# Folding the pooling branch's maps into the output projection's rows, once a layer, instead of a product in each tile

## The chip, the cores and the metric

The kernel runs on 1 core of one Trainium2 chip. The metric is the device time of one execution in microseconds (us). The program works in f32 throughout; TensorE's records show each f32 matmul (and each transpose, which is a matmul with the identity) as two instructions.

## The reference, cut to what matters

Two layers work on 2048 tokens of width 1024. In each, the normalised input is projected to 2048 columns, of which 256 (`u_b`) belong to the pooling branch. Three branches give a vector `mix` of 1024 channels (512 attention, 256 pooling, 256 retention), and `w_out` maps it back:

```python
def multiscale_pool(u, pool_w, pool_scale):
    ...
        mean = (c - shifted) / jnp.minimum(t1, float(w))
        outs.append(mean - uf[..., sl])
    d = jnp.stack(outs, axis=2)
    y = jnp.einsum('bsgc,gce->bsge', d, pool_w.astype(jnp.float32)).reshape(b, s, POOL_WIDTH)
    return (y * pool_scale.astype(jnp.float32)).astype(u.dtype)
...
        mix = jnp.concatenate([y_a, y_b, y_c], axis=-1)
        x = x + jnp.einsum('bse,ed->bsd', mix, w_out[l])
        x = x + moe_ffn(rms_norm(x, norm_ffn[l]), router_w, router_b, w_gate[l], w_up[l], w_down[l])
```

`pool_w` holds four 64x64 maps a layer, `pool_scale` 256 numbers. Between `d` and the sum over `w_out`'s rows 512 to 767 all is linear, so map and scale can also be multiplied into those rows. `moe_ffn` sends each token to 2 of 32 experts.

## The kernel before, in words

A layer has a mixing part and an expert part. The mixing part takes the tokens in 16 tiles of 128 and is a software pipeline written out by hand: `steps` runs `step(s, b, front, back, tail)` for s = 0 to 17. `front` is tile s (input projection, in four chunks of 512 columns), `back` is tile s-1 (attention, pooling, retention, output projection), `tail` is tile s-2 (router). Steps 0, 1, 14, 15, 16 and 17 are written out, steps 2 to 13 are a loop of two. Step 0 has no back, step 16 no front, step 17 only a tail. Each engine runs its own program in its written order, and semaphores tie them together; a wait holds all that stands behind it on that engine.

On TensorE (L1059 to L1248) a step issues, in order: transposes of q, k and the retention's rows; chunk 0; scores; transposes for the router; chunk 1; the first half of chunk 2; L1171 to L1191, the retention's products and the pooling sums (`d` of the reference, transposed, in `bB[:, 256:512]`); the second half of chunk 2; L1198, transposes of the attention's probabilities; L1203, the pooling map, two matmuls; the first half of chunk 3; L1216, probabilities by values; L1220, transposes of `yc`; the second half of chunk 3; L1239, the output projection, in two halves k of eight matmuls of 128x512, over the blocks `d` of `mixT` and `wout`. Blocks 4 and 5 are the pooling branch. Between the two halves stand the router's rank products and the transposes of the next tile's normalised input (`hn_transposes`).

On ScalarE (L612 to L672) the order around the change is: L655 (third chunk out of PSUM), L659 (transposed probabilities), L663 (mapped pooling, with the scale, into `mixT[:, 4:6]`, which raises `pool_ready`), L667 (fourth chunk), L670 (attention into `mixT[:, 0:4]`, which raises `attn_ready`), L672 (sum of squares). On VectorE L826 copies the pooling sums from PSUM to `dT` and raises `kvd_read`.

`par` holds a layer's small parameters, with the maps `pw` (L187, two blocks of 128x128 with two maps each on the diagonal) and the scale `pscale`. `wout` (L182) has a layer's whole `w_out`, loaded during step 0. The PSUM banks are `bA` to `bF` and `bIP0`, `bIP1`; the projections use the last two, the rest of a step the others.

Of the kernel before, what the change touches and what calls it, by code (L numbers as in the profile page):

```python
# [21 lines left out]
P = 128  # L22
# [31 lines left out]
ALU = mybir.AluOpType  # L54
# [80 lines left out]
def small_parameters(norm_mix, norm_ffn, q_norm, k_norm, sinks, pool_w, pool_scale, router_w, router_b):  # L135

    both = lambda a: np.concatenate([a, a], 1)[:, :, None]
    per_chunk = lambda a: a.reshape(DEPTH, -1, P).transpose(0, 2, 1)

    heads = sinks.reshape(DEPTH, 2, 2, 2).transpose(0, 2, 3, 1)  # L140
    heads = np.broadcast_to(heads[:, :, None, :, :, None], (DEPTH, 2, 64, 2, 2, 2)).reshape(DEPTH, P, 8)
    maps = np.zeros((DEPTH, 2, 64, 2, 2, 64), pool_w.dtype)
    for g in range(4):
        maps[:, g % 2, :, g // 2, g % 2] = pool_w[:, g]
    maps = maps.reshape(DEPTH, P, 2 * P)
    router = np.broadcast_to(router_w.reshape(DC, P, NE).transpose(1, 0, 2).reshape(1, P, DC * NE), (DEPTH, P, DC * NE))
    bias = np.broadcast_to(router_b.reshape(1, 1, NE), (DEPTH, P, NE))
    return np.ascontiguousarray(np.concatenate(
        [per_chunk(norm_mix), per_chunk(norm_ffn), both(q_norm), both(k_norm), heads, maps,
         per_chunk(pool_scale), router, bias, by_quarters(norm_ffn, 1).reshape(DEPTH, P, DC)], 2))  # L150


def program(nc, x, small, w_in, w_out, w_gate, w_up, w_down, consts_d, rot_d, pads_d, out):
# [4 lines left out]
    with ExitStack() as ctx:  # L158
# [47 lines left out]
        def part(phase, n):  # L206
            at = used[phase]
            used[phase] = at + n
            assert used[phase] <= ARENA, used
            return arena[:, at:at + n]  # L210
# [16 lines left out]
        v0w = [part("mix", 128) for _ in range(2)]  # L227
        upv = [part("mix", 256) for _ in range(2)]
        iT = part("mix", 512).rearrange("p (h n) -> p h n", h=4)
        dT = part("mix", 256).rearrange("p (j n) -> p j n", j=2)  # L230
        logits4 = dT[:, 0]
        state = [part("mix", 128).rearrange("p (j e) -> p j e", j=2) for _ in range(2)]
        kv = part("mix", 128).rearrange("p (j e) -> p j e", j=2)
        ysq, z = (part("mix", 256).rearrange("p (a j e) -> p a j e", a=2, j=2) for _ in range(2))
# [32 lines left out]
        inner_ready, pe_h2T, h2T_ready, pe_router = sem("inner_ready"), sem("pe_h2T"), sem("h2T_ready"), sem("pe_router")  # L267
        pe_ykv, kvd_read, ysq_ready, z_ready = sem("pe_ykv"), sem("kvd_read"), sem("ysq_ready"), sem("z_ready")
        exp_gate, silu_ready, yc_ready = sem("exp_gate"), sem("silu_ready"), sem("yc_ready")
        pe_pT, pT_ready, pe_lin, pool_ready = sem("pe_pT"), sem("pT_ready"), sem("pe_lin"), sem("pool_ready")  # L270
        pe_ycT, ycT_ready, pe_pv, attn_ready = sem("pe_ycT"), sem("ycT_ready"), sem("pe_pv"), sem("attn_ready")
        vw_ready = sem("vw_ready")
        pe_oproj, x_new = sem("pe_oproj"), sem("x_new")
# [322 lines left out]
        def _(e):  # L596
# [6 lines left out]
            with e.Fori(0, DEPTH) as l:  # L603
# [8 lines left out]
                def step(s, b, front, back, tail):  # L612
                    t0 = l * TILES + s
                    o = 1 - b
                    if back:

                        e.wait_ge(pe_qkrT, t0)
                        for g in range(2):
                            a(qT[:, g].rearrange("p c j n -> p j c n"),
                              bC[:, 256 * g:256 * g + 256].rearrange("p (j c n) -> p j c n", j=2, c=2), ACT.Copy, scale=qgs[:, 0:1])  # L620
                        a(kTr[:, :, :, o], bD[:, 0:256].rearrange("p (g c n) -> p g c n", g=2, c=2), ACT.Copy,
                          scale=kg).then_inc(qkT_ready, 1)
                        e.wait_ge(proj_ready, t0 * 4)
                        a(eg, proj[o][:, RG0:RG0 + RW], ACT.Exp, scale=-1.0).then_inc(exp_gate, 1)
                    if front:
                        if has_next(s):
                            e.wait_ge(hn_ready, t0 + 1)
                            sumsq_front(s + 1, o)
                        e.wait_ge(proj_psum, t0 * 4 + 1)
                        a(proj[b][:, 0:512], bIP0[:, :], ACT.Copy).then_inc(proj_ready, 1)  # L630
                    if back:

                        e.wait_ge(neg_max, t0)
                        for k in range(2):
                            for g in range(4):
                                n = 4 * k + g
                                a(pr[:, k, g], (bC, bD)[k][:, g * P:(g + 1) * P], ACT.Exp, bias=stat[:, 16 + n:17 + n],  # L637
                                  scale=1.0, accum_out=stat[:, 24 + n:25 + n])
                        a(stat[:, 40:48], stat[:, 32:40], ACT.Exp).then_inc(exp_done, 1)
                    if front:  # L640
                        e.wait_ge(proj_psum, t0 * 4 + 2)
                        a(proj[b][:, 512:1024], bIP1[:, :], ACT.Copy).then_inc(proj_ready, 1)
                    if tail:
                        e.wait_ge(pe_parts, t0 - 1)
                        a(logits4, bA[:, 0:P], ACT.Copy).then_inc(parts_read, 1)
                        e.wait_ge(pe_router, t0 - 1)
                        a(es, bA[:, 256:288], ACT.Exp, scale=-1.0).then_inc(exp_router, 1)
                    if back:
                        e.wait_ge(pe_ykv, t0)
                        for k in range(2):  # L650
                            a(ysq[:, k], (bE, bF)[k][:, 256:384].rearrange("p (h e) -> p h e", h=2), ACT.Square)
                        e.drain().then_inc(ysq_ready, 1)
                    if front:
                        e.wait_ge(proj_psum, t0 * 4 + 3)
                        a(proj[b][:, 1024:1536], bIP0[:, :], ACT.Copy).then_inc(proj_ready, 1)  # L655
                    if back:
                        e.wait_ge(pe_pT, t0)
                        for k in range(2):
                            a(prT[:, k].rearrange("p g n -> p (g n)"), (bC, bD)[k][:, :], ACT.Copy)  # L659
                        e.drain().then_inc(pT_ready, 1)  # L660
                        e.wait_ge(pe_lin, t0)
                        for j in range(2):
                            a(mixT[:, 4 + j], bB[:, j * P:(j + 1) * P], ACT.Copy, scale=pscale[:, j:j + 1])  # L663
                        e.drain().then_inc(pool_ready, 1)
                    if front:
                        e.wait_ge(proj_psum, t0 * 4 + 4)
                        a(proj[b][:, 1536:2048], bIP1[:, :], ACT.Copy).then_inc(proj_ready, 1)  # L667
                    if back:
                        e.wait_ge(pe_pv, t0)
                        a(mixT[:, 0:4].rearrange("p j n -> p (j n)"), bF[:, :], ACT.Copy).then_inc(attn_ready, 1)  # L670
                        e.wait_ge(x_new, t0 * 2)
                        a(squares, xr[o], ACT.Square, accum_out=stat[:, 4:5]).then_inc(sumsq_2, 1)  # L672
# [33 lines left out]
        def _(e):  # L706
# [38 lines left out]
            with e.Fori(0, DEPTH) as l:  # L745
                e.wait_ge(par_full, (l + 1) * 16)

                v.tensor_scalar(qgs[:, :], qg, HD ** -0.5, None, ALU.mult)
                v.tensor_copy(base[:, :], const("slot0"))
                v.memset(state[0], 0.0)  # L750
# [17 lines left out]
                def step(s, b, front, back, tail):  # L768
# [53 lines left out]
                    if back:  # L822

                        e.wait_ge(pe_ykv, t0)
                        v.tensor_tensor(kv, bB[:, 0:128].rearrange("p (j e) -> p j e", j=2), state[o], ALU.add)
                        v.tensor_copy(dT, bB[:, 256:512].rearrange("p (j n) -> p j n", j=2))  # L826
                        e.drain().then_inc(kvd_read, 1)
                        v.tensor_tensor(state[b], kv, bc(const("gamma").unsqueeze(2), [P, 2, HD]), ALU.mult)

# [216 lines left out]
        def _(e):  # L1046
# [8 lines left out]
            with e.Fori(0, DEPTH) as l:  # L1055
# [3 lines left out]
                def step(s, b, front, back, tail):  # L1059
# [39 lines left out]
                    if not front:  # L1099

                        e.wait_ge(rank_read, t0 - 1)
                        e.wait_ge(pool_ready, t0 - 1)
                    if back:

                        if not first:
# [88 lines left out]
                    if back:  # L1194
# [3 lines left out]
                                i = tr((bC, bD)[a][:, g * P:(g + 1) * P], pr[:, a, g])  # L1198
                        i.then_inc(pe_pT, 1)

                        wait_alone(e, kvd_read, t0)
                        for j in range(2):
                            i = mm(bB[:, P * j:P * j + P], pw[:, j], dT[:, j], start=True, stop=True)  # L1203
                        i.then_inc(pe_lin, 1)
                    chunk(3, (0, 4))
                    if back:
                        e.wait_ge(pT_ready, t0)
# [17 lines left out]
                    if back:  # L1225

                        e.wait_ge(wout_full, (l + 1) * 16)
                        e.wait_ge(pool_ready, t0)
                        for k in range(2):
                            if front:  # L1230
                                e.wait_ge(proj_ready, t0 * 4 + 3 + k)
                            elif k == 0:
                                e.wait_ge(x_new, (t0 - 2) * 2 + 2)
                            for n, d in enumerate((4, 5, 0, 1, 2, 3, 6, 7)):
                                if n == 2 and k == 0:
                                    e.wait_ge(attn_ready, t0)
                                if n == 6 and k == 0:
                                    e.wait_ge(ycT_ready, t0)
                                i = mm(bIP[k][:, :], mixT[:, d], wout[:, d, 512 * k:512 * k + 512], start=(n == 0), stop=(n == DC - 1))  # L1239
                            i.then_inc(pe_oproj, 1)  # L1240
                            if k == 0 and tail:
# [76 lines left out]
```

## Time and profile before

| what | us |
|---|---|
| median of 3 runs | 3396.63 (3395.2 to 3398.5) |
| the profiled execution | 3395.41 |
| its span, first to last instruction | 3393.6 |
| TensorE busy | 3236.3 (95%) |
| VectorE busy | 1483.2 (44%) |
| GpSimd busy | 1086.7 (32%) |
| ScalarE busy | 579.8 (17%) |
| mean granted TensorE clock | 0.974 of 2.4 GHz |

All rows come from one execution. L numbers are lines of the kernel before. PE is TensorE, PEld its weight loads, DVE VectorE, ACT ScalarE, POOL GpSimd. Matmuls overlap their neighbours in the records, so what a group costs is the distance from its start to the next group's start, not its own duration.

### The profile page before, as it was taken

The numbers are of one execution on the slowest core, as the hardware profiler recorded it, in microseconds if no ns is written. First come the engines' busy times: TensorE is split into PE (matmuls) and PEld (weight loads), VectorE is DVE, ScalarE is ACT, GpSimd is POOL, SyncE is SP. The second block draws the span as 40 slices with busy tenths as digits, with TensorE's granted clock in tenths as the row PEclk, the third lists the DMA queues.
The fourth block names the chain that finished last, engine by engine and source line by source line (L and its number), as shares of the span: only waits on it lengthen the run. The fifth ranks groups of instructions, "written<-read, shape, count | busy, mean of one in ns | idle before, by whom it ended". The sixth has DMA issues, their size and how long they took to land.

```text
span 3393.6 us, 57969 instructions
## 1 busy us (share of the span) xinstructions
PE 3236.3 (95%) x19892; PEld 2437.0 (72%) x19892; DVE 1483.2 (44%) x4776; ACT 579.8 (17%) x1728; POOL 1086.7 (32%) x1093
## 2 busy tenths in 40 slices
PE   8999999999499999999889999999994999999998
PEld 4555555555399999999845555555553999999998
DVE  3566666666322222222235666666663222222221
ACT  1212122122011111111112121222220111111111
POOL 1011111111155455554410111111111554555643
PEclk9999999999699999999989999999996999999999
DMA  6101111011288899999831011010122888999996
GB/s 260 57 29 56 45 39 56 28 56 61 105 306 289 281 319 328 343 345 344 279 120 57 29 56 56 28 56 35 50 78 107 298 287 283 323 331 340 342 345 189
DMA packets 209896, 596.94 MB, mean 176 GB/s; under 512 B 61368, under 2 KB 101816, under 8 KB 176696
## 3 DMA queue, kind: packets, MB, share of 16 engines
q1 hardware_dynamic: 146904, 510.75, 39.7%
q0 software_dynamic: 62720, 82.95, 11.2%
q8 instruction: 124, 2.03, 0.2%
q14 instruction: 148, 1.21, 0.1%
HBM read 514.37 MB, written 80.35 MB: 175 GB/s over the span
## 4 chain that ended last, share of the span: by engine, by line
PE 91%; DVE 2%; DMA 2%; issue 2%; POOL 1%; DVEq 1%; ACT 0%; SPq 0%; POOLq 0%; ACTq 0%
PE bank L1264 27%; PE bank L1077 26%; PE bank L1290 14%; PE bank L1239 13%; PE bank L1052 4%; DMA arena<-hrows,arena 1%; PE bank L1191 1%; PE bank L1216 1%; PE bank L1135 1%; POOL arena L570 1%; POOL out L577 1%; PE bank L1144 1%; PE bank L1159 1%; DVE arena L1005 0%; DMA out<-arena 0%
## 5 line engine op out<-in xcount | busy, mean ns | idle before, releaser
L1264 PE MATMUL bank<-arena,wts 128*128 128x135 f32 (+6 forms) x8192 | 1026.0, 287 | 45.2 <-DVE arena L1008 45.2
L1264 PEld LDWEIGHTS bank<-arena,wts 128*128 128x128 f32 x8192 | 1019.7, 191 | 45.5 <-issue 45.5
L1077 PE MATMUL bank<-wts,arena 128*128 128x512 f32 x2048 | 916.8, 596 | 3.6 <-DVEq L763 3.6
L1077 PEld LDWEIGHTS bank<-wts,arena 128*128 128x128 f32 x2048 | 376.3, 191 | 416.0 <-issue 412.2
L577 POOL DMA_INDIRECT out<-arena x316 | 512.8, 1623 | 148.3 <-issue 89.9
L1290 PE MATMUL bank<-arena,wts 128*128 128x135 f32 (+6 forms) x4096 | 516.6, 287 | 2.6 <-DVE arena L1032 2.4
L1290 PEld LDWEIGHTS bank<-arena,wts 128*128 128x128 f32 x4096 | 509.3, 190 | 4.7 <-issue 4.6
L1239 PE MATMUL bank<-wts,arena 128*128 128x512 f32 x1024 | 453.4, 596 | 0.0
L1005 DVE STREAM_TRANSPOSE arena<-arena 128x256 f32<-128x256 f32 x316 | 140.9, 446 | 571.1 <-DMA arena<-hrows,arena 551.2
L570 POOL DMA_INDIRECT arena<-hrows,arena x316 | 306.5, 970 | 190.1 <-issue 168.5
L1239 PEld LDWEIGHTS bank<-wts,arena 128*128 128x128 f32 x1024 | 193.2, 191 | 230.6 <-issue 221.5
L511 POOL TENSOR_TENSOR arena<-arena 128x256 f32<-128x256 f32 x32 | 23.1, 721 | 958.1 <-DVEq L837 958.1
L1019 DVE STREAM_TRANSPOSE arena<-bank 128x480 f32<-128x480 f32 (+4 forms) x192 | 104.2, 594 | 469.6 <-PE bank L1290 469.6
L687 ACT ACTIVATE arena<-arena,tab 128x256 f32<-128x256 f32 x316 | 133.0, 496 | 600.5 <-DVEq L1020 600.5
L546 POOL DMA_INDIRECT table<-pay,sloti x64 | 63.7, 995 | 482.4 <-DVE sloti L952 472.6
L1052 PE MATMUL bank<-cst,arena 128*128 128x128 f32 x1152 | 163.6, 285 | 47.5 <-DVE arena L755 36.0
L1052 PEld LDWEIGHTS bank<-cst,arena 128*128 128x128 f32 x1152 | 136.6, 147 | 91.0 <-issue 52.6
L565 POOL TENSOR_TENSOR arena<-tab,quarter 128x5 int32<-128x5 int32 (+2 forms) x64 | 12.2, 191 | 420.8 <-DMA tab<-table 389.5
L695 ACT ACTIVATE arena<-bank 128x270 f32<-128x270 f32 (+6 forms) x64 | 26.3, 411 | 691.5 <-PE bank L1264 691.5
L672 ACT ACTIVATE arena<-arena 128x1024 bf16<-128x1024 f32 x32 | 33.8, 1057 | 469.7 <-DVE arena L867 469.7
L867 DVE TENSOR_TENSOR arena<-arena,bank 128x512 f32<-128x512 f32 x64 | 44.0, 688 | 125.7 <-PE bank L1239 115.5
L637 ACT ACTIVATE arena<-bank,stat 128x128 f32<-128x128 f32 x256 | 89.7, 379 | 31.3 <-DVEq L797 31.0
(163 smaller groups left out, 2346.8 us busy)
## 6 DMA issues: line engine op xcount, KB each, us to landing
wts<-in_w_gate SPq DMA_DIRECT2D x128, 1024.0 KB, 5.2
wts<-in_w_up SPq DMA_DIRECT2D x128, 1024.0 KB, 7.2
wts<-in_w_down SPq DMA_DIRECT2D x128, 1024.0 KB, 15.4
hrows<-arena SPq DMA_DIRECT2D x36, 512.0 KB, 2.9
out<-arena SPq DMA_DIRECT2D x36, 512.0 KB, 2.6
arena<-in_x SPq DMA_DIRECT2D x32, 512.0 KB, 4.7
wts<-in_w_in SPq DMA_DIRECT2D x8, 2048.0 KB, 16.0
arena<-out SPq DMA_DIRECT2D x32, 512.0 KB, 4.8
```

What stands on the lines that cost most here:

```text
L546: e.indirect_dma_start(table, bass.IndirectOffsetOnAxis(ap=sloti[b][:, k:k + 1].bitcast(U32), axis=0), pay[b][:, 2 * k:2 * k + 2], None).t ...
L570: e.indirect_dma_start(xg[b][:, g * PIECE:(g + 1) * PIECE], None, hpieces, bass.IndirectOffsetOnAxis(ap=piece[:, i, g:g + 1].bitcast(U32), ...
L577: e.indirect_dma_start(opieces, bass.IndirectOffsetOnAxis(ap=piece[:, i, g:g + 1].bitcast(U32), axis=0), ysb[b][:, g * PIECE:(g + 1) * PIE ...
L637: a(pr[:, k, g], (bC, bD)[k][:, g * P:(g + 1) * P], ACT.Exp, bias=stat[:, 16 + n:17 + n], scale=1.0, accum_out=stat[:, 24 + n:25 + n])
L687: a(y, y, ACT.Copy, scale=tab[:, i, g, 1:2].bitcast(F32)).then_inc(y_scaled, 1)
L1005: v.transpose(windows(xT_all[b], g * step, DC, 32 * GMAX, 32), x_piece)
L1019: v.transpose(y[:, 3 * k:3 * k + m], windows(bk, 0, m, w, w))
L1052: return nc.tensor.transpose(dst, src, ident[0:m, 0:m])
L1077: i = mm(bIP[n % 2][:, :], hT[:, d], win[:, n, d], start=(d == 0), stop=(d == DC - 1))
L1239: i = mm(bIP[k][:, :], mixT[:, d], wout[:, d, 512 * k:512 * k + 512], start=(n == 0), stop=(n == DC - 1))
L1264: return mm(gu_at(f, k, w), lhs, xT[:, d, 0:w], start=start, stop=(d == DC - 1), skip_group_check=True)
L1290: j = mm(dst, lhs, hTm[:, f, 0:w], start=(f == 0 and d % 3 == 0), stop=(f == FC - 1), skip_group_check=True)
```

## The change

The host lays the maps out transposed. At a layer's start VectorE multiplies `pw` by the scale, row by row. In step 1, ahead of the first output projection, TensorE multiplies the maps into blocks 4 and 5 of `wout` (four matmuls of 128x512 into `bA` to `bD`), and ScalarE copies the four results over those blocks. Step 1 takes the blocks in another order, 4 and 5 last. In each tile the two map matmuls and ScalarE's two scaled copies are gone: VectorE writes the pooling sums straight into `mixT[:, 4:6]`, and TensorE waits for `kvd_read` ahead of the output projection.

```diff
-        maps[:, g % 2, :, g // 2, g % 2] = pool_w[:, g]
+        maps[:, g % 2, :, g // 2, g % 2] = pool_w[:, g].swapaxes(1, 2)
...
-        dT = part("mix", 256).rearrange("p (j n) -> p j n", j=2)
-        logits4 = dT[:, 0]
+        logits4 = part("mix", P)
...  ScalarE
-                        e.wait_ge(pe_lin, t0)
-                        for j in range(2):
-                            a(mixT[:, 4 + j], bB[:, j * P:(j + 1) * P], ACT.Copy, scale=pscale[:, j:j + 1])
-                        e.drain().then_inc(pool_ready, 1)
+                        if isinstance(s, int) and s == 1:
+
+                            e.wait_ge(pe_fold, l + 1)
+                            for j in range(2):
+                                for k in range(2):
+                                    a(wout[:, 4 + j, 512 * k:512 * k + 512], (bA, bB, bC, bD)[2 * j + k][:, :], ACT.Copy)
+                            e.drain().then_inc(fold_ready, 1)
...  VectorE
+                v.tensor_tensor(pw, pw, bc(pscale.unsqueeze(2), [P, 2, P]), ALU.mult).then_inc(maps_ready, 1)
...
-                        v.tensor_copy(dT, bB[:, 256:512].rearrange("p (j n) -> p j n", j=2))
+                        v.tensor_copy(mixT[:, 4:6], bB[:, 256:512].rearrange("p (j n) -> p j n", j=2))
...  TensorE
-                        e.wait_ge(pool_ready, t0 - 1)
+                        e.wait_ge(kvd_read, t0 - 1)
...
-                        wait_alone(e, kvd_read, t0)
-                        for j in range(2):
-                            i = mm(bB[:, P * j:P * j + P], pw[:, j], dT[:, j], start=True, stop=True)
-                        i.then_inc(pe_lin, 1)
...
-                        e.wait_ge(pool_ready, t0)
+                        wait_alone(e, kvd_read, t0)
+                        if first:
+                            e.wait_ge(maps_ready, l + 1)
+                            for j in range(2):
+                                for k in range(2):
+                                    i = mm((bA, bB, bC, bD)[2 * j + k][:, :], pw[:, j], wout[:, 4 + j, 512 * k:512 * k + 512],
+                                           start=True, stop=True)
+                            i.then_inc(pe_fold, 1)
...
-                            for n, d in enumerate((4, 5, 0, 1, 2, 3, 6, 7)):
-                                if n == 2 and k == 0:
+                            for n, d in enumerate((0, 1, 2, 3, 6, 7, 4, 5) if first else (4, 5, 0, 1, 2, 3, 6, 7)):
+                                if d == 0 and k == 0:
                                     e.wait_ge(attn_ready, t0)
-                                if n == 6 and k == 0:
+                                if d == 6 and k == 0:
                                     e.wait_ge(ycT_ready, t0)
+                                if d == 4 and k == 0 and first:
+                                    e.wait_ge(fold_ready, l + 1)
```

## Rows read from the trace of the kernel before

**Rows 1.** The page's busy times, and its chain that ended last, by engine.
```profile
PE 3236.3 (95%) x19892; PEld 2437.0 (72%) x19892; DVE 1483.2 (44%) x4776; ACT 579.8 (17%) x1728; POOL 1086.7 (32%) x1093
...
PE 91%; DVE 2%; DMA 2%; issue 2%; POOL 1%; DVEq 1%; ACT 0%; SPq 0%; POOLq 0%; ACTq 0%
```

**Rows 2.** Waits of PE: waiter, releaser, total us, times, longest us.
```profile
PE bank L1264 <- DVE arena L1008: 45.2, 2, 22.7
PE bank L1052 <- DVE arena L755: 36.0, 2, 21.5
...
PE bank L1290 <- DVE arena L1032: 2.4, 6, 0.7
```

**Rows 3.** Timeline of PE, layer 0, step 1: start, duration, line, instructions merged.
```profile
75.23 0.61 PE L1203 MATMUL bank<-arena,par 128*128 128x128 f32 x4
75.67 3.60 PE L1077 MATMUL bank<-wts,arena 128*128 128x512 f32 x8
...
80.50 3.60 PE L1077 MATMUL bank<-wts,arena 128*128 128x512 f32 x8
83.94 7.03 PE L1239 MATMUL bank<-wts,arena 128*128 128x512 f32 x16
90.81 1.04 PE L1052 MATMUL bank<-cst,arena 128*128 128x128 f32 x8
```

**Rows 4.** Timeline of ACT: layer 0's start, step 1, and one row of step 16.
```profile
8.48 1.28 ACT L608 ACT_TABLE_LOAD   x1 [8.48 <-DMA par<-in_small]
...
75.43 1.09 ACT L659 ACTIVATE arena<-bank 128x512 f32<-128x512 f32 x2 [0.28 <-PE bank L1052]
76.61 0.63 ACT L663 ACTIVATE arena<-bank,par 128x128 f32<-128x128 f32 x2
84.14 0.60 ACT L667 ACTIVATE arena<-bank 128x512 f32<-128x512 f32 x1 [6.90 <-PE bank L1077]
84.63 0.59 ACT L670 ACTIVATE arena<-bank 128x512 f32<-128x512 f32 x1
...
837.06 0.47 ACT L621 ACTIVATE arena<-bank,par 128x256 f32<-128x256 f32 x1
```

**Rows 5.** Timeline of DVE: start of either layer, and step 1 of layer 0.
```profile
10.95 0.15 DVE L722 TENSOR_SCALAR newton<-stat 128x1 f32<-128x1 f32 x1 [2.16 <-ACT arena L608]
...
71.27 0.41 DVE L826 COPY arena<-bank 128x256 f32<-128x256 f32 x1
...
1704.24 0.15 DVE L722 TENSOR_SCALAR newton<-stat 128x1 f32<-128x1 f32 x1 [12.17 <-ACT arena L608]
```

**Rows 6.** Groups of DVE by line and form: count, busy us, mean ns, idle before.
```profile
L811 DVE TENSOR_TENSOR arena<-arena 128x256 f32<-128x256 f32 x32 | 13.6, 426 | 2.6
```

**Rows 7.** Timeline of PE, layer 0, step 16 (no chunks).
```profile
837.59 1.16 PE L1135 MATMUL bank<-arena 64*128 64x128 f32 x16 [1.96 <-ACT arena L621]
840.86 1.22 PE L1144 MATMUL bank<-arena 64*128 64x128 f32 x8 [2.11 <-DVE arena L775]
...
855.23 1.06 PE L1203 MATMUL bank<-arena,par 128*128 128x128 f32 x4
858.74 1.97 PE L1216 MATMUL bank<-arena 128*64 128x128 f32 x16 [2.45 <-DVEq L837]
...
861.13 8.58 PE L1239 MATMUL bank<-wts,arena 128*128 128x512 f32 x16
```

**Rows 8.** Busy time in stretches of 1 us; behind POOL: granted PE clock, DMA, GB/s.
```profile
839.00:840.00 1.00, 0.00 (x0) 0.00 (x0) 0.80 (x2) 0.00 (x0) 0.00 (x0) 1.00 0.00 0
840.00:841.00 1.00, 0.14 (x2) 0.17 (x3) 0.71 (x2) 0.00 (x0) 0.00 (x0) 0.67 0.00 0
...
864.00:865.00 1.00, 1.00 (x3) 0.39 (x3) 0.77 (x4) 0.00 (x0) 0.00 (x0) 0.88 0.00 0
```

**Rows 9.** Longest pieces of the chain that ended last: first two experts, layer 0.
```profile
923.18 21.38 PE bank L1264 x128
953.88 18.24 PE bank L1264 x128
```

More of the change, by code:

```diff
@@ L269, in program @@
         exp_gate, silu_ready, yc_ready = sem("exp_gate"), sem("silu_ready"), sem("yc_ready")
-        pe_pT, pT_ready, pe_lin, pool_ready = sem("pe_pT"), sem("pT_ready"), sem("pe_lin"), sem("pool_ready")
+        pe_pT, pT_ready, maps_ready, pe_fold, fold_ready = sem("pe_pT"), sem("pT_ready"), sem("maps_ready"), sem("pe_fold"), sem("fold_ready")
         pe_ycT, ycT_ready, pe_pv, attn_ready = sem("pe_ycT"), sem("ycT_ready"), sem("pe_pv"), sem("attn_ready")
```

## The prediction

> **What bounds the kernel now.** I first read the page for busy times and the chain that ended last: TensorE is busy 95% of the span and holds 91% of the chain [rows 1]. So a microsecond counts only if it is taken from TensorE, or put before it. The table of waits then tells where TensorE stands still. Its longest entries come twice, once a layer, at the start and the end of a layer's expert part; none comes more than 6 times in 32 tiles [rows 2]. The tile in full flow, with a new tile's projection (chunks) between the parts of the old one, therefore has no wait on TensorE at all: what TensorE executes there is the time. The timeline of the first such tile (step 1) shows the pieces around the change: two pooling matmuls (four instructions, since each f32 matmul is recorded as two), half a chunk, the second half of chunk 3, then the output projection L1239 [rows 3]. ScalarE is done with its pooling copies at 77.24 and then idles 6.90 us until chunk 3 ends [rows 4].
>
> **Removed from each tile.** Between the starts of L1203 and of the chunk behind it lie 75.67 - 75.23 = 0.44 us [rows 3]; I take 0.445. That is the price, not the recorded 0.61 us, which overlaps its neighbour. It is saved where TensorE runs without gaps: steps 1 to 15 of each layer, 30 in all, 30 x 0.445 = 13.4 us. Step 16 has no chunk; there L1203 begins at 855.23 and lasts 1.06 us, then TensorE idles 2.45 us for VectorE's normalisation L837 before L1216 [rows 7]. That wait becomes 1.06 us longer: no gain. Bounds for the two such steps: 0, and 2 x 1.06 = 2.1 us if L837 came earlier too; it waits for nothing that the change removes, so 0.
>
> ScalarE loses two copies of 128x128 and a drain (0.62 us a tile), but its next work, L667, waits for TensorE to end chunk 3, 6.90 us later. `attn_ready` then comes at the same place, at 85.22, after L670. Two pairs of matmuls of the pooling rows (4 x 0.43 = 1.72 us from 83.94, so to 85.66) cover it as before [rows 3, 4]. Nothing is gained there, nothing lost: the cover would have to shrink by 0.44 us to open a wait. VectorE's copy from PSUM to `dT` becomes the same copy to `mixT`, 0.41 us on either side [rows 5]. TensorE's wait for it moves from ahead of L1203 to ahead of L1239, 12.3 us after that copy was done in step 1, so it costs nothing; the `pool_ready` wait goes with its work. No DMA and no queue of SyncE or GpSimd changes.
>
> **Added at a layer's start.** VectorE multiplies the maps by the scale, 128x256 f32: by L811, of the same size, 0.43 us [rows 6]. In layer 0 it stands where VectorE idles 2.16 us until 10.95 for ScalarE's square, which itself waits for a table load of 1.28 us [rows 5, 4]. In layer 1 VectorE idles 12.17 us for the same [rows 5]. Cost 0; without that cover it would be 2 x 0.43 = 0.9 us.
>
> **Added in step 1 of each layer, on the path.** Let F be the time where L1239 would begin.
> 1. The fold: four matmuls of 128x512 f32, eight instructions. Sixteen of them take 90.81 - 83.94 = 6.87 us, eight take 83.94 - 80.50 = 3.44 us; their recorded end is 3.60 us after the first start [rows 3].
> 2. The new order of L1239 begins with `d` = 0, which needs `attn_ready`; no other work of TensorE stands between fold and that wait. On ScalarE the fold's copies stand ahead of L667 and L670, and wait for the fold's last matmul. ScalarE starts 0.04 us after the recorded end (chunk 3: 84.10 to 84.14), at F + 3.64. Two copies of 128x512 and a drain take 76.61 - 75.43 = 1.18 us, each further copy 84.63 - 84.14 = 0.49 us: four take 2.16 us. Then L667 0.49 us and L670 0.59 us: `attn_ready` at F + 6.88 [rows 3, 4].
> 3. TensorE starts 0.06 us after its releaser ends (L621 ends at 837.53, L1135 starts at 837.59) [rows 4, 7]: F + 6.94.
> So each layer pays 6.94 us, 3.44 of matmuls and 3.50 of waiting, of which 3.34 us show as idle. Two layers: 13.9 us. `fold_ready` itself, behind six pairs of matmuls, is never late. What stands behind TensorE's wait are L1239, the transposes of the next tile and VectorE's residual add L867; all shift together, and the next tile has no wait to absorb it.
>
> The two sums almost cancel: 13.9 - 13.4 = +0.5 us.
>
> **The clock.** The stall has a second price. In step 16 TensorE idled 1.96 us, worked 1.16 us, idled 2.11 us [rows 7], and its granted clock, 2.4 GHz until then, shows 0.67 as the mean of 840 to 841, that is, it fell to 1.2 GHz within that microsecond [rows 8]. After the 1.96 us alone it had not fallen. An idle stretch of 3.34 us between dense matmuls lies above the one and near the sum of the two, so I take it that it falls. What a fall costs once dense work resumes: L1239's first sixteen in step 16 take 8.58 us, where the same sixteen at full clock take 7.03: 1.55 us [rows 7, 3], the clock being back within 864 to 865 [rows 8]. The upper row is the first expert's 128 matmuls, 21.38 against 18.24 us: 3.14 us [rows 9]. Nearest in kind is the first, the same L1239: 2 x 1.55 = 3.1 us. Bounds: 0 and 2 x 3.14 = 6.3 us.
>
> The Trainium skill, TensorE: Matmul & The Clock Gate, section "Why this matters for your kernels", speaks against this change here: it asks that no idle gap be left between bursts of matmuls, since the engine then returns to its half clock. By that rule the stall is punished once in each layer, which gives the +3.6 us below; without it the sum stays at +0.5 us.
>
> **The sum.** -13.4 + 13.9 + 3.1 = +3.6 us. The profiled execution took 3395.4 us for a span of 3393.6, 1.2 us under the median of 3396.6 shown. So the profile after should be about 3399.0, and the median 3396.6 + 3.6 = 3400.2 us. The spread of the runs shown is 3.3 us, so a shift of less than 0.2% (6.8 us) is what I call no difference.
>
> **The rivals.**
> *The clock holds through the stall.* The fall before came after two idle stretches, 4.07 us in all; 3.34 us may fall short. Then +0.5 us, 3397.1. Chance 0.25. Small variants of this come from the tail of a layer, where falls and returns of the clock may shift by a microsecond or two with everything ahead of them.
> *The clock stays low longer.* For it speaks the first expert's row, and that the falls are at the mercy of where the stall lies; then each layer pays 3.14 us or more: 0.5 + 6.3 = +6.8 us, 3403.4, at the edge of measurably slower; with a ScalarE that takes 0.6 us a copy instead of 0.49, 8 x 0.11 = 0.9 us more. Chance 0.20.
> *Other side: the stall is hidden.* If the eviction lay under matmuls, the layers would pay 2 x 3.44 = 6.9 us only: 6.9 - 13.4 = -6.5 us, 3390.1; it is measurably faster from the point where a tile also yields 0.46 us or more instead of 0.445. For it speaks only that L1239's old order covered `attn_ready`; against it, that the new order in step 1 names `d` = 0 first, and that `pe_fold` is raised once, after the last matmul. Chance 0.07.
> *The change doesn't do what it says*, in that a tile's 0.445 us is not returned (a wait opens in the flowing tile): up to 13.4 us are lost, +17 us, 3413.6. Against it: VectorE and ScalarE both idle microseconds around the spot [rows 4, 5]. Chance 0.05.
> The forecast, two stalls of 3.5 us and a short fall of the clock in each layer (or in one alone), has 0.43.
>
> **How the numbers follow.** Forecast 3400.2. Leaving out the hidden stall and the lost tile leaves 0.88; trimmed at the ends of the other cases by the spread of the runs (3397.1 - 3.3 and 3403.4 + 3.3, a little beyond), the range is 3393 to 3407. Faster by over 0.2%: the hidden stall with its upper variants, 0.06. Slower by over 0.2% (3403.4 and above): half of the longer fall, the lost tile and a little of the forecast, 0.19. The same: 0.75.
>
> **What would show it.** In the profile after: no L1203 in the tiles, and transposes followed at once by a chunk; the tile in full flow 0.44 to 0.45 us shorter; in step 1 eight instructions of 128x512 for about 3.44 us, then TensorE idle for 3.3 us with ScalarE's L670 as releaser, twice; four ScalarE copies of 128x512 at a pitch of 0.49 us; the clock at 1.2 GHz for a few microseconds around or behind the stall. The prediction is wrong if the idle stretch is under 2 us, if the clock stays down more than 7 us, or if a wait shows up 30 times in the tiles.

## The result, and the profile after

The changed kernel takes 3403.38 us (median of 17 runs, 3401.39 to 3408.96); before takes 3396.63 us (17 runs, 3394.07 to 3399.81). The ratio is 1.002, 95% interval 1.0013 to 1.0028: 6.75 us more, at the very edge of the 0.2% (6.8 us) that the prediction called a difference. The forecast was +3.6 us (3400.2 us); the measured time lies inside its range of 3393 to 3407 us. The profiled execution's span is 3400.7 us, 7.1 us over [rows 1]'s. The page has:

```profile
span 3400.7 us, 57631 instructions
...
PE 3230.2 (95%) x19780; PEld 2423.9 (71%) x19780; DVE 1480.8 (44%) x4778; ACT 564.5 (17%) x1672; POOL 1088.0 (32%) x1093
```

TensorE has 112 instructions fewer than in [rows 1]: 128 of L1203 gone, 16 of the fold come. Among the waits of TensorE, against [rows 2], one row is new, L1247 (L1239 before) on ScalarE's L672, and the last one shown (L1290 before, in the expert part) has grown from 2.4 us:

```profile
PE bank L1215 <- DVEq L840: 7.4, 2, 4.1
PE bank L1247 <- ACT arena L672: 7.0, 2, 3.5
...
PE bank L1298 <- DVE arena L1035: 5.7, 8, 1.4
```

Step 1 of layer 0 on TensorE's timeline, against [rows 3]; the number in brackets is the idle time before the row:

```profile
75.23 1.04 PE L1055 MATMUL bank<-cst,arena 128*128 128x128 f32 x8
76.10 3.60 PE L1080 MATMUL bank<-wts,arena 128*128 128x512 f32 x8
...
84.37 3.60 PE L1232 MATMUL bank<-wts,par 128*128 128x512 f32 x8
91.46 8.67 PE L1247 MATMUL bank<-wts,arena 128*128 128x512 f32 x16 [3.50 <-ACT arena L672]
99.97 1.04 PE L1055 MATMUL bank<-cst,arena 128*128 128x128 f32 x8
```

The transposes are followed at once by the chunk; L1203 is gone. From the fold's start to the output projection 7.09 us pass (6.94 forecast), and TensorE idles 3.50 us of them (3.34 forecast). The first half of the output projection then takes 99.97 - 91.46 = 8.51 us, where 6.87 us were usual: 1.64 us lost. ScalarE in the same place, against [rows 4]:

```profile
88.00 2.06 ACT L665 ACTIVATE wts<-bank 128x512 f32<-128x512 f32 x4 [10.61 <-PE bank L1232]
90.23 0.60 ACT L669 ACTIVATE arena<-bank 128x512 f32<-128x512 f32 x1 [0.16 <-issue]
90.72 0.59 ACT L672 ACTIVATE arena<-bank 128x512 f32<-128x512 f32 x1
```

The attention's copy L672 stands behind four copies of the fold and chunk 3's; `attn_ready` comes at 91.31 (90.72 + 0.59), and TensorE starts 0.15 us later. The stretches of 1 us (fields as in [rows 8]: the granted clock is the third number from the end) show where the 1.64 us come from:

```profile
90.00:91.00 1.00, 0.00 (x0) 0.00 (x0) 0.00 (x0) 0.84 (x3) 0.00 (x0) 1.00 0.00 0
91.00:92.00 1.00, 0.54 (x1) 0.50 (x2) 0.00 (x0) 0.31 (x1) 0.00 (x0) 0.60 0.00 0
92.00:93.00 1.00, 1.00 (x2) 0.34 (x1) 0.00 (x0) 0.00 (x0) 0.00 (x0) 0.50 0.00 0
93.00:94.00 1.00, 1.00 (x2) 0.34 (x1) 0.00 (x0) 0.00 (x0) 0.00 (x0) 0.50 0.00 0
94.00:95.00 1.00, 1.00 (x3) 0.52 (x2) 0.00 (x0) 0.00 (x0) 0.00 (x0) 0.69 0.00 0
95.00:96.00 1.00, 1.00 (x3) 0.39 (x3) 0.00 (x0) 0.00 (x0) 0.00 (x0) 1.00 0.00 0
```

The clock fell from 2.4 to 1.2 GHz near the end of the idle stretch, at about 91.2 us, and was back before 95 us. Layer 1 is alike: 3.50 us idle, 1.48 us lost.

### The profile page after: what moved, and what is told of

Same layout as the page of the kernel before. It is cut to its first block, busy times and chain, and to the rows that moved or that the text cites. A ratio compares the mean times of both kernels' runs of the same rounds, so it can differ in the third digit from the quotient of the medians.

```text
span 3400.7 us, 57631 instructions
## 1 busy us (share of the span) xinstructions
PE 3230.2 (95%) x19780; PEld 2423.9 (71%) x19780; DVE 1480.8 (44%) x4778; ACT 564.5 (17%) x1672; POOL 1088.0 (32%) x1093
## 4 chain that ended last, share of the span: by engine, by line
PE 89%; DVE 3%; DMA 3%; issue 2%; POOL 1%; DVEq 1%; ACT 1%; SPq 0%; ACTq 0%; POOLq 0%
PE bank L1080 26%; PE bank L1272 26%; PE bank L1298 15%; PE bank L1247 13%; PE bank L1055 4%; DMA arena<-hrows,arena 2%; PE bank L1194 1%; PE bank L1215 1%; PE bank L1138 1%; DVE arena L1008 1%; POOL arena L569 1%; PE bank L1147 1%; PE bank L1162 1%; PE bank L1186 0%; PE bank L1188 0%
## 5 line engine op out<-in xcount | busy, mean ns | idle before, releaser
L1298 PE MATMUL bank<-arena,wts 128*128 128x135 f32 (+6 forms) x4096 | 516.7, 287 | 5.8 <-DVE arena L1035 5.7
L1298 PEld LDWEIGHTS bank<-arena,wts 128*128 128x128 f32 x4096 | 509.3, 190 | 7.9 <-issue 7.6
L1247 PE MATMUL bank<-wts,arena 128*128 128x512 f32 x1024 | 455.6, 598 | 7.1 <-ACT arena L672 7.0
L1247 PEld LDWEIGHTS bank<-wts,arena 128*128 128x128 f32 x1024 | 193.7, 192 | 239.8 <-issue 221.7
```

Of the source, the lines that this page charges most:

```text
L1298: j = mm(dst, lhs, hTm[:, f, 0:w], start=(f == 0 and d % 3 == 0), stop=(f == FC - 1), skip_group_check=True)
```

## The experiments

Each kernel was timed beside before. Where two other kernels are compared, the difference is that of their medians on the same chip; one trace of each kernel was kept.

**The changed kernel again**, with no edit.

> The changed kernel unchanged, as the yardstick of this chip and a second profile. Its sum, step by step from the two traces: +17.3 us in the two steps 1 (2 x 7.1 us of fold and stall, 1.64 and 1.48 us of low clock), -13.4 us in the thirty flowing tiles, about -1 us in the two steps 16: near +3 us. The profile showed +7.1 us, the rest of it in the first tile's clock (0.9 us) and in the expert parts (about 3 us). Theory A: that rest is scatter of one execution, and a new profile puts it elsewhere; the median then is 3399 to 3401 us. Theory B: the expert parts have become slower with the change, by VectorE's L1035 coming later; the waits of L1298 on it are again 5 to 6 us in the profile (2.4 before), and the median is 3403 us.

3404.56 us (11 runs; before 3396.33), ratio 1.0025 (1.0016 to 1.0034). So the change costs 7 to 8 us and not the 3 to 5 us of theory A: the rest is no scatter of one execution. Theory B gets the median, and the waits of L1298 are 5.4 us again, but that is no proof: the two other traces of before show 4.3 and 5.1 us for the same wait, so the 2.4 us of [rows 2] were the lowest of three. The profile has the same stall of 3.50 us in layer 0 and a longer spell of low clock:

```profile
90.71 10.12 PE L1247 MATMUL bank<-wts,arena 128*128 128x512 f32 x16 [3.50 <-ACT arena L672]
100.67 1.04 PE L1055 MATMUL bank<-cst,arena 128*128 128x128 f32 x8
```
```profile
94.00:96.00 2.00, 2.00 (x4) 0.71 (x3) 0.00 (x0) 0.00 (x0) 0.00 (x0) 0.50 0.00 0
96.00:98.00 2.00, 2.00 (x5) 0.87 (x4) 0.00 (x0) 0.00 (x0) 0.00 (x0) 0.80 0.00 0
```

9.96 us in place of 6.87: 3.09 us lost, with the clock back only after 96 us. The same stall can cost 1.5 or 3.1 us.

**The fold's copies behind the attention's copy.**

```diff
-                        if isinstance(s, int) and s == 1:
-                            e.wait_ge(pe_fold, l + 1)
-                            ...   four copies, fold_ready
                     if front:
                         e.wait_ge(proj_psum, t0 * 4 + 4)
                         a(proj[b][:, 1536:2048], bIP1[:, :], ACT.Copy).then_inc(proj_ready, 1)
                     if back:
                         e.wait_ge(pe_pv, t0)
                         a(mixT[:, 0:4].rearrange("p j n -> p (j n)"), bF[:, :], ACT.Copy).then_inc(attn_ready, 1)
+                        if isinstance(s, int) and s == 1:
+                            e.wait_ge(pe_fold, l + 1)
+                            ...   four copies, fold_ready
```

> ScalarE's four copies of the fold are moved behind its copy of the attention (L672), so attn_ready comes under the fold's matmuls and the copies lie under the six pairs of matmuls of blocks 0 to 3, 6 and 7. If the stall is what the change pays for, TensorE shows no idle time ahead of L1247 in step 1 and the clock does not fall there: 2 x 3.50 + 1.64 + 1.48 = 10.1 us less than the changed kernel, 3393.3 us, about 3 us under before (ratio 0.999). If the price sits in the fold's matmuls or elsewhere, the gain is under 3 us.

3393.57 us (11 runs), ratio 0.9991 (0.9982 to 1.0): 11.0 us less than the changed kernel beside it, where 10.1 us were expected. TensorE's and ScalarE's timelines of step 1:

```profile
84.12 3.60 PE L1231 MATMUL bank<-wts,par 128*128 128x512 f32 x8
87.55 7.03 PE L1246 MATMUL bank<-wts,arena 128*128 128x512 f32 x16
94.42 1.04 PE L1054 MATMUL bank<-cst,arena 128*128 128x128 f32 x8
```
```profile
84.32 0.60 ACT L662 ACTIVATE arena<-bank 128x512 f32<-128x512 f32 x1 [7.18 <-PE bank L1079]
84.81 0.59 ACT L665 ACTIVATE arena<-bank 128x512 f32<-128x512 f32 x1
87.75 2.06 ACT L670 ACTIVATE wts<-bank 128x512 f32<-128x512 f32 x4 [2.35 <-PE bank L1231]
```

The output projection follows the fold 3.43 us after its start, with no bracket and at full clock (6.87 us for its first half). The four copies end at 89.81, ahead of blocks 4 and 5.

**The pooling map left out.** No fold matmuls, no fold copies, the old order of blocks; the output lacks the pooling branch's map and scale.

> The fold is left out, its matmuls and its copies, and step 1 has the old order of blocks: the pooling branch's map and scale are not applied at all. What is left is the tile's part of the change alone. By the forecast: 30 x 0.445 = 13.4 us under before, plus up to 1 us from step 16: 3382.3 to 3383.2 us (ratio 0.996). Rival, that part of the tile's saving is given back in the expert parts or in the tiles: 3386 us or more.

4985.6 us: no answer to the question. The branch without its map changes the router's input, and the expert part, whose number of rounds depends on the data, runs twice as many rounds; its first matmul line counts:

```profile
L1256 PE MATMUL bank<-arena,wts 128*128 128x135 f32 (+6 forms) x16384 | 2050.3, 287 | 115.5 <-DVE arena L1004 115.5
```

The count is 8192 in the other kernels. The question went to the next but one experiment, which keeps the values.

**Fillers in the stall.**

```diff
                                 e.wait_ge(proj_ready, t0 * 4 + 3 + k)
+                                if first and k == 0:
+                                    for _ in range(4):
+                                        mm(bIP[0][:, :], pw[:, 0], wout[:, 0, 0:512], start=True, stop=True)
```

> In step 1, between the fold and the output projection, TensorE runs four more matmuls of 128x512 (3.44 us) into a bank that the output projection then overwrites; they fill the stall of 3.50 us and cost nothing in themselves. If the clock's fall is a price of its own, it disappears: 1.64 + 1.48 = 3.1 us less than the changed kernel, 3400.3 us. If the fall costs nothing on the whole, the time stays at 3403.4 us; if the fillers cost what they last, it rises by up to 6.9 us.

3399.45 us (11 runs), 5.1 us less than the changed kernel beside it; 3.1 us were expected. Adding 6.9 us of matmuls makes the kernel faster. In its profile the clock does not fall in step 1:

```profile
87.02 3.60 PE L1240 MATMUL bank<-wts,par 128*128 128x512 f32 x8
90.59 7.13 PE L1250 MATMUL bank<-wts,arena 128*128 128x512 f32 x16
97.56 1.04 PE L1055 MATMUL bank<-cst,arena 128*128 128x128 f32 x8
```

The output projection begins hardly earlier relative to the fold (7.00 against 7.09 us), but its first half takes 6.97 us and not 8.4 to 10. So the clock's price is real. Its size can't be read from the 5.1 us: the kept trace is that of the fastest of the 11 executions (3396.41 us), and of its 8.8 us to the trace of the changed kernel beside it 4.6 us lie in the two steps 1 (0.2 of them before the output projection), 2.7 us in the expert parts, which the fillers do not touch.

**The tile's matmuls put back into the changed kernel.**

```diff
                         i.then_inc(pe_pT, 1)
+                        e.wait_ge(kvd_read, t0)
+                        for j in range(2):
+                            mm(bB[:, P * j:P * j + P], pw[:, j], mixT[:, 4 + j], start=True, stop=True)
```

> The changed kernel with the two map matmuls put back into each tile, at their old place and behind their old wait; their result is not read. So it holds the fold, the stall and the tile's old matmuls together: what it costs over the changed kernel is what the tiles save. By the forecast 30 x 0.445 = 13.4 us, up to 14.4 with step 16: 3417 to 3418 us with the changed kernel at 3403.4 to 3404.6. The two changed kernels measured so far lie 4 to 5 us above the sum of their terms. If that rest is a saving that the tiles don't deliver, this kernel costs only some 9 us more, 3413 us; if it sits elsewhere, the full 13 to 14 us show.

3419.73 us (5 runs), ratio 1.0069 (1.0055 to 1.0083), and 14.9 us over the changed kernel with ScalarE's copies (3404.86 us beside it; next but two, equal to the changed kernel). So the tiles deliver about their 13.4 us. What is missing sits elsewhere. Its layer 1 shows one more thing:

```profile
1798.78 7.10 PE L1251 MATMUL bank<-wts,arena 128*128 128x512 f32 x16 [3.49 <-ACT arena L672]
1805.72 1.04 PE L1055 MATMUL bank<-cst,arena 128*128 128x128 f32 x8
```
```profile
1799.00:1800.00 1.00, 1.00 (x3) 0.42 (x3) 0.00 (x0) 0.00 (x0) 0.00 (x0) 1.00 0.00 0
```

The same idle 3.49 us, and the clock stayed at 2.4 GHz: 0.07 us lost.

**The fold's copies made twice.**

```diff
                             e.wait_ge(pe_fold, l + 1)
+                            for again in range(2):
                                 ...   the four copies
+                                if not again:
+                                    e.drain()
```

> ScalarE copies the four results of the fold twice, so the stall of 3.50 us grows by 4 x 0.49 us and a drain, to about 5.5 us in each layer. If the clock's fall lasts as long as it did (one short spell, 1.5 us lost), the time rises by 2 x 2.0 = 4.0 us, to 3408 us. The rival that the clock stays low longer after a longer stall: up to 3.14 us lost in place of 1.5, 3411 us.

3409.86 us (5 runs), 5.0 us over the changed kernel with ScalarE's copies beside it. The stall is 5.63 us, 2.13 us longer:

```profile
93.58 9.42 PE L1250 MATMUL bank<-wts,arena 128*128 128x512 f32 x16 [5.63 <-ACT arena L675]
102.83 1.04 PE L1058 MATMUL bank<-cst,arena 128*128 128x128 f32 x8
```

First half 9.25 and, in layer 1, 9.14 us: 2.38 and 2.27 us lost. A longer stall costs its own length, 2 x 2.13 = 4.3 us, and little more in clock: 2.3 us a layer against a mean of 1.9 us for the shorter stall (below). The time lies between the two that were named, 3408 and 3411 us; the rival's 3.14 us of low clock did not come.

**The kernel before again**, with no edit.

> The kernel before, for a second profile of it. The expert parts took 784.7 and 777.6 us in its first profile, and 785.9 and 778.6 us on average in the profiles with the fold (changed kernel twice, late copies, filler: 783.8 to 786.2, 778.3 to 779.0). If this is scatter, the second profile of before lies within 783.8 to 786.2 and 777.6 to 779.0 as well; if it is an effect of the change it is again at 784.7 and 777.6. Median 3396.3 us.

3397.58 us (11 runs). Its expert part of layer 0 (first matmul of the first expert to layer 1's first transposes) took 783.6 us, under the range of the fold's kernels; layer 1's (to the end) 778.3 us.

**ScalarE's copies put back into the changed kernel's tiles.**

```diff
                         e.drain().then_inc(pT_ready, 1)
+                        e.wait_ge(kvd_read, t0)
+                        for j in range(2):
+                            a(spare, mixT[:, 4 + j], ACT.Copy, scale=pscale[:, j:j + 1])
+                            e.drain()
```

> The changed kernel with two 128x128 copies and drains put back on ScalarE in each tile, at the place of the old ones, into a tile that nobody reads. By the forecast ScalarE's share of the tile was worth nothing, as its next work waits several us for TensorE: no change against the changed kernel, 3403.4 to 3404.6 us. If removing ScalarE's work had been part of the gain, up to 30 x 0.62 = 18.6 us more.

3404.86 us (11 runs), ratio 1.0024 (1.0015 to 1.0033), as the changed kernel's 3404.56 (1.0025). ScalarE's share of the tile was worth nothing: ahead of its next work it still stood idle 6.20 us for TensorE.

**The late copies again**, and three attempts on the missing 3 us.

> The kernel with the late copies again, unchanged: it measured 3393.6 us, 0.9991 of before with an interval that ends at 1.0. Expected 3393.6 us again, so 3 us under before. By the terms (6.9 us of fold, 13.4 us saved) it should be 6.5 us under before; the missing 3 us stand open.

3393.73 us (11 runs; before 3397.56), ratio 0.9989 (0.998 to 0.9998). The two comparisons make it 2.8 and 3.8 us faster than before, small next to the scatter, with one interval that reaches 1.0 and one that ends just under it.

```diff
+                        if k == 1:
+                            for _ in range(8):
+                                e.nop()
                         src = w_down[bass.ds(l, 1), bass.ds(i, 1), k * 256:(k + 1) * 256, :]
```

> The missing 3 us, theory 1. In every kernel with the fold the second expert's gather lands 17.0 to 17.8 us after the first expert's first matmul, in both profiles of before 16.2 to 16.5 us. SyncE issues the four loads of gate and up alike; the two loads of w_down take it 1.33 to 1.67 us in before and 0.96 to 1.04 us in the others. Here eight empty instructions of SyncE stand between the two, in every expert, on top of the late copies. If an earlier second load is what crowds the gather, the gather is back at 16.2 to 16.5 us and the time falls by up to 3 us, to 3390.6 us. If not, the gather stays at 17.2 us and the time at 3393.6 us.

3394.15 us (11 runs), no gain. The experiment missed its aim: the two issues still took 1.02 us, and the trace has no record of an empty instruction (57631 instructions, as without them), so theory 1 is neither shown nor refuted by it. The gather landed at 17.19 us. This trace shows how a late gather can cost more than its wait. TensorE waited 2.42 us for the first expert's hidden values, and then the granted clock was 0.50 from 945 to 948 us, so the 64 instructions took 10.88 us to the next group's start instead of some 9.2 us:

```profile
943.86 11.04 PE L1300 MATMUL bank<-arena,wts 128*128 128x168 f32 x64 [2.42 <-DVE arena L1037]
954.74 5.44 PE L1274 MATMUL bank<-arena,wts 128*128 128x168 f32 x37
```

```diff
+                for _ in range(8):
+                    e.nop()
                 R = read_rounds(e, l)
```

> The missing 3 us, theory 2: it is a matter of where SyncE's instructions lie in memory, and not of the change. On top of the late copies, SyncE has eight empty instructions ahead of the expert part, where it waits anyway, so all its later instructions lie elsewhere. If the place decides, the gather's landing moves from 17.2 us (either way) and the two w_down issues take another time than 1.0 us; if not, both stay and the time is 3393.6 us.

> The same eight empty instructions in the kernel before. If the place of SyncE's instructions decides, before loses its advantage: the gather lands at 17.0 us or later, the w_down issues take about 1.0 us, and the time rises by 2 to 3 us, to 3399 us. If not, the gather stays at 16.2 to 16.5 us and the time at 3396.6 us.

3394.34 us and 3397.64 us (11 runs each): no change in either. The gather stayed at 17.24 us with the late copies and at 16.52 us in before, the w_down issues at 1.02 and 1.52 us. But the empty instructions are not in these traces either (57631 and 57969 instructions, as without them), so nothing shows that SyncE's code moved, and theory 2 stays open too.

The row that stays different, VectorE's first transpose of the second expert's tokens, which waits for their gather; before again, then the late copies again:

```profile
939.20 3.05 DVE L1005 STREAM_TRANSPOSE arena<-arena 128x256 f32<-128x256 f32 x6 [16.75 <-DMA arena<-hrows,arena]
```
```profile
937.52 3.05 DVE L1007 STREAM_TRANSPOSE arena<-arena 128x256 f32<-128x256 f32 x6 [17.39 <-DMA arena<-hrows,arena]
```

TensorE's rows of the first expert, in the same order:

```profile
922.70 21.34 PE L1264 MATMUL bank<-arena,wts 128*128 128x168 f32 x128 [22.71 <-DVE arena L1008]
944.31 9.36 PE L1290 MATMUL bank<-arena,wts 128*128 128x168 f32 x64 [0.27 <-DVE arena L1032]
```
```profile
920.38 21.28 PE L1271 MATMUL bank<-arena,wts 128*128 128x168 f32 x128 [22.68 <-DVE arena L1010]
942.62 2.66 PE L1297 MATMUL bank<-arena,wts 128*128 128x168 f32 x17 [0.97 <-DVE arena L1034]
```

So the transposes begin 16.50 us after the first matmul in before and 17.14 us after it with the late copies. VectorE, in its written order, does the second expert's tokens ahead of the first expert's hidden values, so TensorE waits 0.97 us for those instead of 0.27 us.

## Why the prediction was right or wrong

**Tiles, -13.4 us: right, a little less in fact.** Between the router products of neighbouring steps lie 52.50 or about 52.82 us in before and 52.06 or about 52.37 us after: 0.42 to 0.47 us a tile in most pairs, as little as 0.19 us in a few. The 28 tiles between step 1 and step 16, both layers together, give 12.0 us, 0.43 us each, so thirty give some 12.8 us. With the matmuls put back the same stretches take 745.9 us each again, as in before. That step 16 gives nothing was nearly right: TensorE waits 4.13 us (layer 0) and 3.3 us (layer 1) before L1215 in place of 2.45 us [rows 7], so what was freed is idle.

**ScalarE's and VectorE's shares at nothing: right.** The first is shown by its own experiment. The maps' product took VectorE 0.43 us and its idle time shrank from 2.16 to 1.83 us, with layer 0's first matmuls at 14.54 us (14.57 before).

**Fold and stall, +13.9 us: right.** 2 x 7.09 = 14.2 us. `attn_ready` came 6.94 us after the fold's start, 6.88 forecast, and the 0.15 us from there to TensorE's start was taken as 0.06. That the place of ScalarE's copies is the cause of the stall is shown: moved behind L672, the stall and the fall are gone and 11.0 us come back.

**The clock, +3.1 us: the mechanism right, the size low, and the rivals not exclusive.** In the eight stalls of 3.50 us in four profiles (changed kernel twice, ScalarE's copies, tile's matmuls) the loss was 1.64, 1.48, 3.09, 1.53, 2.85, 1.77, 2.93 and 0.07 us (the first half's duration less 6.87 us). The mean is 1.92 us, so 3.8 us for two layers where 3.1 us were forecast. The sizes come in steps: the clock stayed low for about 3.4 us where 1.5 to 1.8 us were lost, for about 6.8 us where 2.9 to 3.1 us were lost (and in both stalls of 5.63 us), and not at all where 0.07 us were lost. In all of these the loss is, within 0.1 us, half of the low time that fell on matmuls; in the stretches above, low from 91.2 to 94.6 us with matmuls from 91.46 us, that is 1.6 us. What I had written as three cases with chances, the clock holds, falls briefly, stays low longer, all occur with the same instructions and the same stall; only their mean belongs in the sum. Over both layers of one execution the four traces lost 3.0 to 4.6 us. The Trainium skill, TensorE: Matmul & The Clock Gate, section "Why this matters for your kernels", asks for no idle gaps between bursts of matmuls. The fillers agree (no fall in their trace, 5.1 us won on the median by adding work); the one stall of eight that cost nothing shows that a gap of this size does not always bring the fall.

**The term that was missing: the expert parts, about +2.7 us.** The change does not touch them, and the prediction gave them no term: it held that no DMA changes and that all behind the stall shifts together. With before, before again and before with empty instructions they took 784.3 us (layer 0, 783.6 to 784.7) and 778.0 us (layer 1, 777.6 to 778.3) on average; in the ten profiles of kernels with the fold 786.1 us (783.8 to 787.9) and 778.9 us (778.0 to 780.0). The ranges of a layer overlap, but both layers together take 1561.9 to 1562.7 us in the first group and 1564.5 to 1566.0 us in nine of the ten; the tenth, the fillers' trace, has 1562.1 us. So of the size I am less sure than of the sign. What goes with it in every profile, in both layers, is the second expert's gather: 16.2 to 16.5 us after the first matmul in before's three, 17.0 to 17.8 us in the other ten. TensorE's first matmul on the hidden values moves with it, from 21.3 to 21.6 us after the first matmul to 22.1 to 22.9 us, 0.9 us a layer on average. That is 1.8 of the 2.7 us. In two of the ten (the one shown above, and the tile's matmuls put back), in layer 0, the clock fell once more after that wait, and these have the longest expert parts, 787.9 us. SyncE's two `w_down` issues take 1.3 to 1.7 us in the first group and 0.95 to 1.1 us in most of the second. Why a kernel with the fold has this is open: the three experiments with empty instructions reached neither the place of SyncE's instructions nor the delay between the loads. VectorE's and TensorE's code changed in length as well; that was not tried.

The account: +14.2 (fold, stall) + 3.8 (clock) - 12.8 (thirty tiles) - 0.3 (from the scores of step 16 to the first expert, 85.5 against 85.3 us on average, twice) + 2.7 (expert parts) = +7.6 us. Measured: +6.75 us, and +8.2 us in the second comparison. The -0.3 us is within the scatter of its own term, and the expert part of a layer scatters by up to 4 us from profile to profile. That the measured time lies in the range is in part luck: the range was wide for the sake of the clock, and the 2.7 us that the prediction had at nothing are most of the 3.2 us by which it missed.

**The rival of the hidden stall** had its size right for another kernel: 6.9 - 13.4 = -6.5 us. It measured 2.8 and 3.8 us faster; the same 2.7 us of the expert parts are what is missing.

## What to carry to other kernels

Work hoisted out of a loop is paid where it lands: count not only its matmuls but also what the copies of its results out of PSUM are queued ahead of. Here four copies of 0.49 us stood in front of the one copy that the next matmuls needed, and moving them two instructions down turned a loss of 7 to 8 us into a gain of 2.8 to 3.8 us. A stall of TensorE amid dense work has a second price in the clock, one that changes from run to run; put its mean in the sum, and where the stall can't be removed, useless matmuls in it can pay (here 5.1 us). An ablation that changes values is no ablation in a kernel whose trip counts depend on them.

## What the runs showed of the hardware that was not expected

The clock's answer to one and the same idle stretch, 3.50 us between dense f32 matmuls of 128x512, ranged from no fall (0.07 us lost) over a low spell of about 3.4 us (1.5 to 1.8 us lost) to one of about 6.8 us (2.9 to 3.1 us lost); two idle stretches of 5.63 us were followed by low spells of about 6.8 us and lost 2.3 to 2.4 us, since more of the spell lay in the idle time. The second expert's gather landed 16.2 to 16.5 us after the first expert's first matmul in three traces of before and 17.0 to 17.8 us after it in ten traces of kernels that issue the same DMAs; the cause was not found.
